# Moving three steps of a gated linear recurrence between ScalarE and VectorE

## What is computed

```python
u_x = centred_dwconv(h_x @ w_rec, conv_w, conv_b)      # 4 taps; the same for the context
r = sigmoid(einsum('btnk,nkj->btnj', ub, w_a) + b_a)   # a 256x256 matrix for each block
i = sigmoid(einsum('btnk,nkj->btnj', ub, w_i) + b_i)
log_a = -LRU_C * softplus(-lam) * r
a = exp(log_a)
bx = sqrt(-expm1(2 * log_a)) * (i * u)
h_t = a_t * h_{t-1} + bx_t                             # forward and backward in time
y = (gelu(h_x @ w_gate) * (rec_x[0] + rec_x[1])) @ w_out
```

## Time and profile before

| | |
|---|---|
| time, median of 3 runs | 1869.79 us (1866.89 to 1871.46) |
| the profiled execution | 1865.63 us, span of its instructions 1863.9 us |
| busy share of the span | TensorE 89%, VectorE 61%, ScalarE 47% |
| mean granted TensorE clock | 0.936 |
| the LRU stage in the span | about 711 to 905 us |

### The profile page before, as it was taken

The page is one execution under the profiler, slowest core; times in us unless marked ns, Lnnn a source line. Parts: engine busy times, 40 slices in busy tenths (PEclk is TensorE's granted clock), DMA queues, the critical chain, the costliest instruction groups (busy, mean ns, idle before and its releaser), DMA issues.

```text
span 1863.9 us, 24508 instructions
## 1 busy us (share of the span) xinstructions
PE 1654.6 (89%) x8874; PEld 1350.4 (72%) x8874; DVE 1134.5 (61%) x1819; ACT 875.0 (47%) x1398; POOL 10.8 (1%) x32
## 2 busy tenths in 40 slices
PE   3999889999999998995699997788868898999998
PEld 1864457888888896784599996766656876877767
DVE  2345654644444466899636666566555667777875
ACT  3234555522223255886534445335233456656563
POOL 1000000000000000000000000000000000000000
PEclk9999999999999998998759998789979799999999
DMA  8277732422332322322235663323110478878784
GB/s 322 73 302 265 257 138 56 138 89 90 98 103 91 97 73 69 101 91 68 90 113 158 189 190 118 112 91 104 55 46 23 147 246 286 271 257 280 248 292 164
DMA packets 201835, 279.72 MB, mean 150 GB/s; under 512 B 12315, under 2 KB 111117, under 8 KB 195597
## 3 DMA queue, kind: packets, MB, share of 16 engines
q1 hardware_dynamic: 200064, 269.90, 45.1%
q0 software_dynamic: 1152, 8.39, 1.1%
q10 hardware_dynamic: 524, 0.19, 0.0%
HBM read 277.40 MB, written 1.05 MB: 149 GB/s over the span
## 4 chain that ended last, share of the span: by engine, by line
PE 59%; DVE 19%; DMA 10%; ACT 8%; issue 3%; ACTq 0%; DVEq 0%; SPq 0%; POOL 0%; POOLq 0%
PE bank L392 48%; DMA stage<-in_w_dram 9%; DVE weights_lo L365 5%; ACT weights_hi L353 3%; PE bank L629 2%; PE bank L1186 1%; PE bank L1170 1%; PE bank L1562 1%; PE bank L1154 1%; DMA work<-in_c_ctx_dram 1%; DVE work L2475 1%; DVE work L2438 1%; DVE turn L2466 1%; DVE work L2485 1%; PE bank L1612 1%
## 5 line engine op out<-in xcount | busy, mean ns | idle before, releaser
L365 DVE TENSOR_TENSOR weights_lo<-stage,weights_hi 128x1024 fp32r<-128x1024 f32 x428 | 515.9, 1223 | 127.1 <-ACT weights_hi L353 116.4
L353 ACT ACTIVATE weights_hi<-stage 128x1024 fp32r<-128x1024 f32 x428 | 442.0, 1056 | 218.8 <-DMA stage<-in_w_dram 115.6
L392 PE MATMUL bank<-act_hi,weights_hi 128*128 128x256 f32 (+2 forms) x1072 | 349.5, 326 | 35.2 <-DVE act_lo L474 13.4
L392 PE MATMUL bank<-act_lo,weights_hi 128*128 128x256 f32 (+2 forms) x1072 | 346.6, 323 | 0.0
L392 PE MATMUL bank<-act_hi,weights_lo 128*128 128x256 f32 (+2 forms) x1072 | 346.2, 323 | 0.0
L392 PEld LDWEIGHTS bank<-act_hi,weights_hi 128*128 128x128 f32 x1072 | 218.8, 204 | 52.1 <-issue 27.5
L392 PE MATMUL bank<-weights_hi,ff_hi 128*128 128x512 f32 x560 | 222.2, 397 | 14.2 <-DVE weights_lo L365 10.6
L392 PE MATMUL bank<-weights_hi,act_hi 128*128 128x512 f32 (+1 forms) x488 | 201.9, 414 | 30.0 <-DVE act_lo L2499 17.5
L392 PEld LDWEIGHTS bank<-act_lo,weights_hi 128*128 128x128 f32 x1072 | 219.0, 204 | 11.3
L392 PEld LDWEIGHTS bank<-act_hi,weights_lo 128*128 128x128 f32 x1072 | 218.7, 204 | 11.3
L392 PE MATMUL bank<-weights_hi,ff_lo 128*128 128x512 f32 x560 | 219.6, 392 | 0.0
(11 more groups left out here) (358 smaller groups left out, 1878.9 us busy)
## 6 DMA issues: line engine op xcount, KB each, us to landing
stage<-in_w_dram SPq DMA_DIRECT2D x192, 512.0 KB, 4.8
stage<-in_mlp_w_dram SPq DMA_DIRECT2D x128, 512.0 KB, 4.0
ada_rows_in<-in_ada_w_dram SPq DMA_DIRECT2D x40, 1024.0 KB, 6.2
stage<-in_w_in_dram SPq DMA_DIRECT2D x32, 512.0 KB, 4.0
stage<-in_lru_w_in_dram SPq DMA_DIRECT2D x20, 512.0 KB, 4.9
ada_rows_in<-in_ada_w_dram POOLq DMA_DIRECT2D x8, 1024.0 KB, 13.4
stage<-in_attn_w_qkv_dram SPq DMA_DIRECT2D x12, 512.0 KB, 4.7
stage<-in_lru_w_out_dram SPq DMA_DIRECT2D x10, 512.0 KB, 4.6
```

What stands on the lines that cost most here:

```text
L353: act.eng.activation(whi[u % NRING][:], stage[u % NSTAGE][:], ACT.Copy).then_inc(sem("hi_ready"), 1)
L365: dve.eng.tensor_tensor(wlo[u % NRING][:], stage[u % NSTAGE][:], whi[u % NRING][:].bitcast(F32), ALU.subtract).then_inc(sem("lo_ready"), 1)
L392: m = pe.eng.matmul(ps, l, r, start=start and j == 0, stop=stop and j == 2, skip_group_check=True)
```

## The change

The rounded copy of u and the square of a go from VectorE to ScalarE, and VectorE does its four i*u products ahead of the rest. In detail:

- ScalarE, in `lru_a`: after two of the four weight roundings it waits for the last tap of each tile of u and writes the rounded copy, two instructions; then the other two weight roundings. All of this is ahead of `lru_b`, in ScalarE's order.
- ScalarE, in `lru_b`: four squares of A into `tbuf`, after the four tanh and ahead of the two weight roundings. Two of them wait until VectorE has read the buffer. The semaphore `tanh` is now raised by the squares.
- VectorE: the taps of both tiles of u, two weight remainders, the two remainders of u, two weight remainders. In `lru_d1` first the four i*u, then the four products that use the square.

```diff
-                split_hi(act, 4)
+                split_hi(act, 2)
+                for m in (0, 1):
+                    s.wait_ge(*act.freed(("rec", n, m)))
+                    s.activation(fhi[:, (n % 2) * 2 + m, :], U[n % 2][:, m, :], ACT.Copy).then_inc(*act.mark("u_hi"))
+                split_hi(act, 2)
 
             def lru_b(n):
...
-                    s.activation(R[:, md, :], R[:, md, :], ACT.Tanh, scale=ncoef[:, c:c + 1]).then_inc(*act.mark("tanh"))
+                    s.activation(R[:, md, :], R[:, md, :], ACT.Tanh, scale=ncoef[:, c:c + 1]).then_inc(*act.mark())
+                for md in range(4):
+                    if md >= 2 or n:
+                        s.wait_ge(sem("ratio"), 4 * n + md - 1)
+                    s.activation(tbuf[:, md % 2, :], A[:, md, :], ACT.Square).then_inc(*act.mark("tanh"))
                 split_hi(act, 2)
...
                     conv_taps(ps, U[n % 2][:, m, :], lambda j: params[:, 2, 10 * j + c_:10 * j + c_ + 1], 4, 2, 2,
                               ("rec", n, m))
+                split_lo(dve, 2)
+                for m in (0, 1):
                     o = (n % 2) * 2 + m
-                    v.tensor_copy(fhi[:, o, :], U[n % 2][:, m, :]).then_inc(*dve.mark())
-                    v.wait_ge(*dve.own())
+                    v.wait_ge(sem("u_hi"), 2 * n + m + 1)
                     v.tensor_tensor(flo[:, o, :], U[n % 2][:, m, :], fhi[:, o, :].bitcast(F32),
                                     ALU.subtract).then_inc(*dve.mark("u_split"))
-                split_lo(dve, 4)
+                split_lo(dve, 2)
 
             def lru_d1(n):
                 for md in range(4):
                     v.wait_ge(*dve.freed(("i", n, md)))
                     v.tensor_tensor(I[:, md, :], I[:, md, :], U[n % 2][:, md // 2, :], ALU.mult).then_inc(*dve.mark("u_used"))
+                for md in range(4):
                     v.wait_ge(sem("tanh"), 4 * n + md + 1)
-                    v.tensor_tensor(tbuf[:, md % 2, :], A[:, md, :], A[:, md, :], ALU.mult).then_inc(*dve.mark())
-                    v.wait_ge(*dve.own())
                     v.scalar_tensor_tensor(out=R[:, md, :], in0=tbuf[:, md % 2, :], scalar=1.0,
                                            in1=R[:, md, :], op0=ALU.add, op1=ALU.mult).then_inc(*dve.mark("ratio"))
                 split_lo(dve, 2)
```

## The result

| | before | changed |
|---|---|---|
| median of 13 runs | 1869.79 us (1863.68 to 1874.38) | 1877.09 us (1873.07 to 1880.61) |
| ratio, 95% interval | | 1.004 [1.0028, 1.0051] |
| span of the profiled execution | 1863.9 us | 1876.1 us |
| LRU stage, first tap to ninth output tile | 714.01 to 903.58: 189.57 us | 716.13 to 913.02: 196.89 us |

The ratio is 5.2 to 9.5 us, and the stage is 7.3 us longer. The two spans differ by more, 12.2 us, since 2.1 us of it lie ahead of the stage and 2.8 behind it, where nothing was changed. The runs of one kernel spread over 10.7 us before and 7.5 us after.

What follows compares the result with a forecast made beforehand. VectorE was taken to bound the LRU stage, with ScalarE's queue behind the waiting copy to lengthen passes. Terms -2.94 + 3.75 + 3.85 + 4.94 - 1.97 = +7.63 us took the median from 1869.79 to 1877.4 us; range 1872 to 1884.

Steps and rivals of the forecast that it cites:

- pass 0, to T(2): LRU stage up to the last convolution tap for pass 2, T(2): comes earlier, -2.94 us.
- passes 1 and 2: LRU passes, each from T to T: 35.45 us instead of 31.70 and 31.60, so +3.75 and +3.85 us.
- pass 3, to the end of its scans: LRU pass 3, from T to its scans' end: 30.80 us against 25.86, so +4.94 us.
- pass 4: Last LRU pass, without a convolution: VectorE's weight remainders end earlier, loads and root product follow as before, -1.97 us.
- sum: All pass terms of the LRU stage together, carried to the kernel's end: +7.63 us.
- The strand from T: From T, the last convolution tap's end for a pass, to VectorE's first product with a square: 15.62 us, against 7.11.
- The table load: A second load in the strand from T: 1.29 us until the next instruction, without the skill page's 1.38 us draining.
- From the product to the root: In a pass, VectorE's first product with a square to its product with the root: 5.82 us instead of 9.39.
- VectorE stays the bound: Rival, 5%: sigmoids still done by T, strand from T VectorE's 8.2 + 0.05 us, sum -14.4, 1855 us.
- Swallowed in the last pass: Rival, 14%: pass 4's loads hang on something earlier than VectorE's remainders, swallowing the delay; sum +3.6, 1873.4 us.
- TensorE on the path: Rival, 7%: TensorE, waiting for late sigmoids' banks, holds gelu past T+31; three passes gain 6 us each, about 1895 us.

Runs made afterwards that it cites:

- 5: The changed kernel with ScalarE's copies of u for passes 1 to 4 each just ahead of the sigmoid that waits for the same tap; 1859.53 us.
- 6: The kernel of 5 with tanh and square of each tile in turn instead of four tanh, then four squares; 1855.51 us.
- experiment 7: The kernel of 5 with pass 4's last two weight roundings behind the roots and VectorE's last two remainders behind the scans; 1855.19 us.
- 2: The kernel before with only the rounded copy of u moved to ScalarE, squares and i*u left as before; 1883.25 us.
- 4: The changed kernel with ScalarE's two rounded copies behind all four weight roundings instead of between them; 1872.65 us.
- experiment 3: The kernel before with only VectorE's four i*u products put ahead of the squares; 1865.64 us.

## Why the prediction was right

| term | predicted | measured in the stage |
|---|---|---|
| pass 0, to T(2) | -2.94 | -3.73 |
| passes 1 and 2 | +3.75, +3.85 | +3.81, +3.90 |
| pass 3, to the end of its scans | +4.94 | +4.97 |
| pass 4 | -1.97 | -1.62 |
| sum | +7.63 | +7.33 |
| time, median | 1877.4 | 1877.09 |

- *The strand from T.* 15.62 us expected, 791.60 - 775.97 = 15.63 measured. A copy is 0.632 us and a square 0.624 (medians of 10 and of 20 rows), a little above the 0.6 taken from the nearest rows, well inside 0.53 to 0.70. The Trainium skill, page "ScalarE: Activation LUTs", section "What ACT_TABLE_LOAD costs", gives 186 ns and 0.833 ns a column for an instruction with immediate scale and bias; worked out from that, an estimate for 512 columns is 613 ns. The trace agrees to about 3%.
- *The table load.* After the newly exposed one, at 778.55, the first sigmoid starts 1.30 us later. The 1.38 us of draining that the same section adds per switch did not show: T to the product would have been 17 us. All 19 table loads of the stage take 1.283 us.
- *From the product to the root.* 5.82 expected, 797.43 - 791.60 = 5.83, with the wait of 0.23 us for the buffer and the 0.46 us before the root product.
- *Pass 0* gained 0.8 us more than I said. VectorE's first weight remainder came 1.41 us earlier after the first tap instead of 1.08, and TensorE's stretch after it was 0.3 us shorter, because it ran at half clock for 3.5 us instead of 4.0 (last section). From T(1) to T(2) another 0.15 went. Before, the second tile's taps started 0.48 us after ScalarE's instruction had ended, now 0.12; why is open.
- *Pass 4* gained 0.35 less. The last load, which I let take the time that it took before, took 5.6 us instead of 5.3.
- *The median.* The sum was right to 0.3 us partly by luck: pass 0 and pass 4 missed in opposite directions, and the interval of the ratio alone is 4.3 us wide. The terms of passes 1 to 3, on which the forecast of a loss rests, each came out within 0.06 us.

The rivals. *VectorE stays the bound* fell: its idle time in a pass went from 0.9 to 8 us. Its price was not far off as a statement of what was there to win: with the copies out of the way (5 and 6) the stage is 10 to 11 us shorter, not 14.4, since ScalarE's strand is then 9.5 us, not VectorE's 8.2. *Swallowed in the last pass* fell: in pass 4 of the changed kernel ScalarE still waits for both loads ahead of its roots, and experiment 7 shows that the roots wait for them, at a price of 6.3 us for the root and 4.0 net. *TensorE on the path* did not come about, at the margin that was named: gelu starts at 803.55, T(2) + 27.6, and the next copy is still 3.11 us early for its tap. ScalarE ahead of the last roots, then TensorE in pass 1:

```profile
897.49 1.06 ACT L353 ACTIVATE weights_hi<-stage 128x1024 fp32r<-128x1024 f32 x1 [2.17 <-DMA stage<-in_lru_w_out_dram]
900.61 1.06 ACT L353 ACTIVATE weights_hi<-stage 128x1024 fp32r<-128x1024 f32 x1 [2.07 <-DMA stage<-in_lru_w_out_dram]
```

```profile
776.03 0.50 PE L392 MATMUL bank<-ff_hi,weights_hi 128*128 128x512 f32 x1 [0.70 <-DVE work L2446]
784.15 0.77 PE L392 MATMUL bank<-act_hi,weights_hi 128*128 128x512 f32 x1 [6.45 <-ACT work L1949]
```

TensorE waits 6.45 us for the banks of the late sigmoids, and its time is hidden. That the loss is the queue's and not the work's was an argument before; experiments 2, 4 and 5 show it.

## What to carry to other kernels

Before an instruction goes to a less busy engine, ask what it waits for and what stands behind it there: a 0.6 us copy that waits for the end of another engine's stretch makes everything queued behind it start then, and here ten of them cost 13.6 us. Put such an instruction where its new engine waits for the same event anyway; the same work then gained 10 us instead of losing 7. And of work taken from the bound engine only what its next waiting partner allows comes through: 9.5 us of ScalarE's strand stood behind VectorE's 8.2.

## What the runs showed beside this

The length of pass 0 up to T(1) varied from 24.3 to 25.4 us between kernels with the same order there (changed, 5, 6, 7), in a stretch where TensorE starts at half clock after a wait. The traces show how: in all four TensorE has been idle for 4.58 us, and its matmuls then come 0.43 us apart at a granted clock of 0.50 to 0.52 (the 1.2 GHz level), before they come 0.23 apart. That slow stretch lasts 3.5 us in the changed kernel and in 7, and 5.6 us in 5 and 6; half of the difference is the 1.0 us. In the kernel before it lasts 4.0 us and in experiment 3 5.65, which is most likely the 0.66 us by which T(1) came later there. What makes it long or short no run here shows. For a change worth a few us this is a third of the effect, and reading the passes behind it apart is what made terms of 0.4 us visible where the measured ratios could not tell them.
